# Hybrid attention/SSD layer on one core: GpSimd subtractions in four pieces, decay rows by a one-hot stationary column, next head pair's projections in the present group's tail

## The reference

```
h   = RMSNorm(x)
p   = h @ w_in          # q-latent 384 | kv-latent 256 | rope key 32 | z 2048 | x,B,C 4096 | dt 32 | gate_a 1024 | gate_b 1024
A   = latent attention: q = RMSNorm(q-latent) @ w_uq (16 heads of 64 + 32 rotary), k, v = RMSNorm(kv-latent) @ w_uk, w_uv,
      causal softmax for the prompt; for the samples over 2048 cached positions
B   = SSD: causal conv of width 4 and SiLU on x, B, C; per head cs = cumsum(dt * a) over chunks of 128 tokens;
      y = (C B^T * exp(cs_l - cs_s), s <= l) @ (x dt) + exp(cs_l) C state;  state = state * exp(cs_end) + B^T exp(cs_end - cs) x dt;
      samples: state = state * exp(dt a) + dt x B, y = C state;  y = RMSNorm(y * SiLU(z)) by groups of 256 channels
mix = (sigmoid(gate_a) * (A @ w_br_attn) + sigmoid(gate_b) * (B @ w_br_ssm)) @ w_out
x   = x + RMSNorm(mix);  x = x + RMSNorm(relu(RMSNorm(x) @ w_up)^2 @ w_down)
```

## Time and profile before

| | |
|---|---|
| median of 3 runs | 1798.62 us |
| the profiled execution: its own time, its span | 1798.48 us, 1796.4 us |
| PE, DVE, ACT, POOL busy | 86%, 56%, 29%, 27% of the span |
| TensorE's mean granted clock | 0.901 |
| opening and group 0 | 0 to 130 us |
| groups 1 to 8 | 130 to 1051 us |
| sample rows | 1051 to 1255 us |
| mixing projections, norms, MLP | 1255 to 1796 us |

### The profile page before, as it was taken

One profiled execution on the slowest core, in us unless ns is written; L12 is line 12 of the kernel. 1 busy time (PEld: TensorE's weight loads), 2 busy tenths in 40 slices (PEclk: granted clock), 3 DMA queues, 4 the chain that ended last, 5 costly groups with the idle time before them and its releaser, 6 DMA issues.

```text
span 1796.4 us, 28368 instructions
## 1 busy us (share of the span) xinstructions
PE 1536.7 (86%) x11696; PEld 1397.6 (78%) x11696; DVE 1005.7 (56%) x1834; ACT 512.5 (29%) x930; POOL 476.6 (27%) x196
## 2 busy tenths in 40 slices
PE   4799879888798888987977668999995899999995
PEld 4798777687787777876867457777995899999995
DVE  6577688688686877877868542333234422222225
ACT  3232323223233233232232222222222322222221
POOL 1232222121221212222112012222344244444441
PEclk9898989899899898998988669999897899999997
DMA  3133121121221211312213028884231222222221
GB/s 107 59 88 95 47 77 59 50 86 51 81 76 39 86 60 39 95 55 72 71 38 96 24 74 275 251 259 132 95 118 35 71 95 92 87 93 95 95 94 60
DMA packets 109586, 160.45 MB, mean 89 GB/s; under 512 B 16497, under 2 KB 83570, under 8 KB 109458
## 3 DMA queue, kind: packets, MB, share of 16 engines
q1 hardware_dynamic: 56594, 130.14, 22.5%
q10 hardware_dynamic: 52864, 28.51, 5.7%
HBM read 145.87 MB, written 12.74 MB: 88 GB/s over the span
## 4 chain that ended last, share of the span: by engine, by line
PE 61%; DVE 28%; issue 5%; ACT 3%; ACTq 2%; SPq 1%; POOL 1%; DMA 1%; DVEq 0%; POOLq 0%
PE lin L455 44%; PE Pb L486 2%; PE lin L494 2%; DVE csm L1294 2%; PE lin L601 2%; PE Pb L542 1%; DVE arena L1273 1%; DVE acc L1469 1%; PE Pb L583 1%; ACTq L1018 1%; PE lin L622 1%; DVE sm L1300 1%; PE Pb L580 1%; PE lin L568 1%; DVE arena L1331 1%
## 5 line engine op out<-in xcount | busy, mean ns | idle before, releaser
L413 POOL TENSOR_TENSOR w_lo<-w_stage,w_hi 128x1024 fp32r<-128x1024 f32 x184 | 464.5, 2525 | 1271.0 <-ACT w_hi L817 1271.0
L455 PE MATMUL lin<-act_hi,w_hi 128*128 128x260 f32 x1760 | 373.2, 294 | 19.6 <-DVE acc L1537 8.1
L455 PE MATMUL lin<-act_lo,w_hi 128*128 128x260 f32 x1760 | 362.4, 288 | 0.0
L455 PEld LDWEIGHTS lin<-act_hi,w_hi 128*128 128x128 f32 x1760 | 279.8, 195 | 28.9 <-issue 21.6
L455 PEld LDWEIGHTS lin<-act_lo,w_hi 128*128 128x128 f32 x1760 | 280.5, 195 | 0.0
L817 ACT ACTIVATE w_hi<-w_stage 128x1024 fp32r<-128x1024 f32 x184 | 193.9, 1054 | 243.1 <-PE lin L455 221.6
L455 PE MATMUL lin<-mid_hi,w_hi 128*128 128x260 f32 x1024 | 220.8, 299 | 41.6 <-DVE mid_lo L1458 18.8
L455 PE MATMUL lin<-act_hi,w_lo 128*128 128x260 f32 x1760 | 235.7, 287 | 0.0
L455 PEld LDWEIGHTS lin<-act_hi,w_lo 128*128 128x128 f32 x1760 | 221.9, 191 | 3.3 <-issue 3.3
L455 PE MATMUL lin<-mid_lo,w_hi 128*128 128x260 f32 x1024 | 216.5, 295 | 0.0
L455 PEld LDWEIGHTS lin<-mid_hi,w_hi 128*128 128x128 f32 x1024 | 168.8, 202 | 52.2 <-issue 32.6
(11 more groups left out here) (240 smaller groups left out, 2139.3 us busy)
## 6 DMA issues: line engine op xcount, KB each, us to landing
w_stage<-in_wall SPq DMA_DIRECT2D x184, 512.0 KB, 3.5
arena<-in_cache SPq DMA_DIRECT2D x124, 144.0 KB, 3.2
arena<-in_state ACTq DMA_DIRECT2D x16, 512.0 KB, 8.3
out_stateT<-arena ACTq DMA_DIRECT2D x16, 512.0 KB, 4.0
o_attn<-in_cache SPq DMA_DIRECT2D x64, 128.0 KB, 3.7
o_attn<-in_cache ACTq DMA_DIRECT2D x64, 128.0 KB, 4.0
arena<-in_xT SPq DMA_DIRECT2D x8, 520.0 KB, 5.4
out_yT<-arena SPq DMA_DIRECT2D x8, 260.0 KB, 2.0
```

The costliest lines, as they stand in the source:

```text
L413: pool.tensor_tensor(w_lo[:, slot, :], w_stage[:, slot, :], w_hi[:, slot, :].bitcast(F32), ALU.subtract).then_inc(S["w_split"], 1)
L455: mm = pe.matmul(lin[:, pl.slot, hf, 0:HALF], w[:, ch.slot, off:off + P], r[:, hf * HALF:(hf + 1) * HALF], start=(k == 0 and p == 0), stop ...
```

## The change

It has three parts.
1. GpSimd's subtraction of a chunk is four instructions of 128 x 256; the signal is on the last.
2. `csm`, `sdm` and their VectorE instructions go. TensorE spreads each head's row itself: the stationary operand is a column of the identity (one-hot over 32 partitions) repeated 128 times, the moving one the 32 x 128 chunk of `cs3`; four such matmuls take the place of the one of 512 columns, and four of 16 columns that of the one of 64.
3. uq0, uq1, uk, uv, ql of the next group stand in the present group's tail, with their chunks UQ and UKV ahead of SA and SB, and so do their read-outs on ScalarE (`heads_out`) and VectorE (`queries_out`, `keys_out`, `latents_out`).

```diff
-STEADY_LIN = HEAD_LIN + ["x0", "sA0", "x1", "bC", "sA1", "b", "sA2", "c", "sA3", "z0", "z1"] + TAIL_LIN
+STEADY_LIN = (["bB", "x0", "sA0", "x1", "bC", "sA1", "b", "sA2", "c", "sA3", "z0", "z1", "uq0", "uq1", "uk", "uv", "bc", "ql"]
+              + S_LIN)
-STEADY_CH = ["UQ", "UKV"] + IN_LIN + ["SA", "SB"]
+STEADY_CH = IN_LIN + ["UQ", "UKV", "SA", "SB"]
...
-                        pool.tensor_tensor(w_lo[:, slot, :], w_stage[:, slot, :], w_hi[:, slot, :].bitcast(F32),
-                                           ALU.subtract).then_inc(S["w_split"], 1)
+                        for q in range(4):
+                            part = slice(256 * q, 256 * q + 256)
+                            low = pool.tensor_tensor(w_lo[:, slot, part], w_stage[:, slot, part],
+                                                     w_hi[:, slot, part].bitcast(F32), ALU.subtract)
+                        low.then_inc(S["w_split"], 1)
...
+                def head_row(h):
+                    return ident[0:32, 4 * g + h:4 * g + h + 1].to_broadcast([32, P])
...
-                    pe.wait_ge(S["csm_ready"], g * 4 + (c + 1))
-                    pe.matmul(lin[:, pl.slot, 0, :], ones[0:32, :], csm[:, :, :], start=True, stop=True)
+                    for h in range(HPG):
+                        pe.matmul(lin[:, pl.slot, 0, h * P:(h + 1) * P], head_row(h), cs3[:, tok], start=True, stop=True)
...
                     values(u + 1)
+                if has_in:
+                    queries()
                 pe.wait_ge(S["o_ready"], g * 8 + 8)
                 pe.wait_ge(S["sqg_ready"], g * 2 + 2)
                 statistics(Pb[0:TOKT, 2, 0:8], sqg, 2).then_inc(S["g_stat"], 1)
+                if has_in:
+                    keys()
+                    value_rows()
                 pe.wait_ge(S["g_diag"], g + 1)
                 broadcast_stat(c_lin(i, "bc"))
+                if has_in:
+                    latent_queries()
...
+                def heads_out():
+                    round_chunk(c_chunk(i, "UKV"))
+                    for h in range(2):
+                        pl = c_lin(i, f"uq{h}")
+                        done(pl)
+                        act.activation(cols(Qt[0:64, h, :]), lin_cols(pl, 0, 64), ACT.Copy)
+                        act.activation(qbd_hi[64 * h:64 * h + 64, 8 * h:8 * h + 8],
+                                       lin[0:64, pl.slot, 1, HALF - NB:HALF], ACT.Copy).then_inc(S["qbd_hi_s"], 1)
+                    pl = c_lin(i, "uk")
+                    round_chunk(c_chunk(i, "UKV").next())
+                    done(pl)
...
-                    if c < NCH - 1:
-                        masked_decay(c + 1)
...
                 if has_in:
-                    z_gate((0,))
+                    z_gate((0, 1))
+                    queries_out(0)
+                    queries_out(1)
                 dve.wait_ge(S["g_stat"], g + 1)
                 inverse_rms(Pb[0:TOKT, 2, 0:8], 0.25 / (D_INNER // GROUPS), S["g_diag"])
                 if has_in:
-                    z_gate((1,))
-                    silu(0)
+                    keys_out()
                 pl = c_lin(i, "bc")
...
                 dve.wait_ge(S["state_out"], g * 16 + 16)
                 if has_in:
+                    latents_out()
+                    silu(0)
                     silu(1)
                     conv(2, 0)
```

More of the change, by code:

```diff
@@ L531, in project, with queries, keys, value_rows @@
                         linear(c_lin(i, name), c_chunk(i, name), K8, act_rhs(), between=between)
+                def queries():
+                    for h in range(2):
+                        linear(c_lin(i, f"uq{h}"), c_chunk(i, "UQ"), [k * 256 + h * P for k in range(3)],
+                               mid_rhs(0, 3), opens=(h == 0))
+                def keys():
+                    linear(c_lin(i, "uk"), c_chunk(i, "UKV"), [0, P], mid_rhs(3, 2))
+                def value_rows():
+                    ch, pl = c_chunk(i, "UKV"), c_lin(i, "uv")
+                    free_slot(pl)
+                    for c in range(NCH):
+                        for k in range(2):
+                            tok = slice(CHUNK * c, CHUNK * (c + 1))
+                            a, b = mid_hi[:, 3 + k, tok], mid_lo[:, 3 + k, tok]
+                            wh = w_hi[:, ch.slot, 512 + k * P:640 + k * P]
+                            wl = w_lo[:, ch.slot, 512 + k * P:640 + k * P]
+                            for n, (x, w) in enumerate(((a, wh), (a, wl), (b, wh))):
+                                mm = pe.matmul(lin[:, pl.slot, 0, c * P:(c + 1) * P], x, w,
+                                               start=(k == 0 and n == 0), stop=(k == 1 and n == 2))
+                    mm.then_inc(S["lin_done"], 1)
+                def latent_queries():
+                    ch, pl = c_chunk(i, "UKV"), c_lin(i, "ql")
+                    free_slot(pl)
+                    pe.wait_ge(S["lin_free"], c_lin(i, "uq1").index + 1)
+                    for k in range(2):
+                        out = lin[:, pl.slot, 0, 16 * k:16 * k + 16]
+                        for n, (w, r) in enumerate(((w_hi, qbd_hi), (w_hi, qbd_lo), (w_lo, qbd_hi))):
+                            mm = pe.matmul(out, w[:, ch.slot, 256 + k * P:384 + k * P], r[:, :],
+                                           start=(n == 0), stop=(n == 2))
+                    mm.then_inc(S["lin_done"], 1)
                 if not has_rest:
@@ L584, in scan_back @@
                               ).then_inc(S["y_done"], 1)
[L586 to L615, removed]
+                if g:
+                    pe.wait_ge(S["state_ready"], g * 4)
+                else:
+                    pe.wait_ge(S["rows_ready"], 1)
+                    pe.wait_ge(S["sp_ln"], 2)
+                for h in range(HPG):
+                    mm = pe.matmul(Pb[:, 3, 16 * h:16 * h + 16], head_row(h), cs3[:, SEQ:SEQ + 16], start=True, stop=True)
+                mm.then_inc(S["sdec_mm"], 1)
                 pe.wait_ge(S["xc_ready"], g * 4 + 4)
@@ L906, in finish_inputs @@
                         act.dma_start(sS[:, t], src.rearrange("b h p n -> (h p) b n")).then_inc(S[f"st_in{t}"], 16)
+                def heads_out():
+                    round_chunk(c_chunk(i, "UKV"))
+                    for h in range(2):
+                        pl = c_lin(i, f"uq{h}")
[6 more added lines that the diff above has]
+                    done(pl)
+                    act.activation(cols(Kt[0:64, 0, :]), lin_cols(pl, 0, 64), ACT.Copy).then_inc(S["k_act"], 1)
+                    pl = c_lin(i, "uv")
+                    done(pl)
+                    act.activation(V[:, 0:2, :], lin[:, pl.slot, 0, 0:256].rearrange("p (c v) -> p c v", c=2), ACT.Copy
+                                   ).then_inc(S["v_act"], 1)
                 if not has_rest:
@@ L916, in group @@
                     finish_inputs()
+                    heads_out()
                     return
@@ L1708, in weight_stream @@
             else:
-                group_rest(name, i - 1)
+                group_rest(name, i if name[0] == "U" else i - 1)
     for m in range(KT):
```

118 lines of the change are left out of this document (51 added, 67 removed).

## The result

The changed kernel takes 1769.91 us (median of 4 runs, 1765.16 to 1772.46) against 1798.3 for the kernel before beside it: ratio 0.9837, 95% interval 0.9803 to 0.9871. The profiled execution took 1770.81 us with a span of 1769.0.

A forecast was written before the change was run, and what follows sets the result against it. TensorE's own work was taken to bound the kernel, with its waits for VectorE to be gained. Terms -20.7 + 16.5 - 1.8 - 3.5 - 5.3 = -14.8 from 1798.5 gave 1784 us; own range 1773 to 1794, wider range 1752 to 1812.

The forecast's parts named there:

- 0.7, my choice: Scan steps: shorter waits leave TensorE's clock up for some more matmuls, 0.7 us a group.
- 0.5 for a clock that falls in the longer wait: Next group's head: TensorE's clock falls while it waits longer behind the late state loads, +0.5 us, six times.
- B: Tail, head and state loads: moved projections make s0 11.5 us later and the second state load 3.3 late; sum +16.5 us.
- C: Group 8, bounded by VectorE: three csm instructions (L1294) go, 0.6 us each, -1.8 us.
- D: Opening and first head: two to three blocks of VectorE, 2.0 to 0.5 us each, shorten; -3.5 us.
- the sums of the branch projection: Head: VectorE's L1273, held 2.78 us, meets a short block instead, -1.5 of TensorE's 2.15 us wait.
- A: Scan steps: TensorE waits less for VectorE once csm goes and holds shorten; -2.95 us a group, times 7, -20.7.
- E: Sample rows: 0.75 us of TensorE's 1.77 us wait behind L1503 goes, for seven rows, -5.3 us.
- Price of a piece: GpSimd's subtraction: a 128 x 256 piece takes 0.72 us, bounds 0.58 and 1.28; four take 2.9 instead of 2.34.
- cheaper tail: Rival, chance 0.25: small instructions of inverse_rms are not held, s0 8.8 us later, second load 0.6 late; 1762 us.
- No change: Rival, chance 0.20: tail takes 2.1 us more per group, so VectorE's savings are waited for at the loads; 1798 us.
- slower case: Rival, chance 0.15: GpSimd's pieces follow so closely that VectorE doesn't get in between; +30, 1829 us.

## Why the prediction was half right

The direction and the mechanisms stood; the sum was off by 13 us. **The step that failed is the price of TensorE's clock**: "0.7, my choice" for it in the scan steps, "0.5 for a clock that falls in the longer wait" in B, and nothing at all in C, D and the sums of the branch projection. A removed wait was priced at little more than its own length, and so was a new one. What the runs showed in its place stands below: 1.7 us a group instead of 0.7 in the scan steps, and 2.0 to 2.4 instead of 0.5 in B, in the other direction.

Without the move, the prediction's own terms are -20.7 - 1.8 - 3.5 - 5.3 - 7 x (1.5 + 1.6) = -53; the kernel without the move measured -61. The move by the same terms is +16.5 + 21.7 = +38; measured +32. By stage, from the two profiled executions:

| stage | forecast | measured |
|---|---|---|
| to the first `scan_front(0)` (D) | -3.5 | -7.4 |
| groups 1 to 7 (A, B) | -4.2 | -11.0 |
| group 8 (C) | -1.8 | -3.5 |
| sample rows and first mixing norm (E) | -5.3 | -6.9 |
| behind it | 0 | +1.6 |
| sum (rounded) | -14.8 | -27.3 |

**Price of a piece.** Right: 0.72 forecast; in the changed kernel the shortest of 736 takes 0.712 us and the median 0.735. GpSimd's own mean per chunk went to 3.1 us, and TensorE hardly waited for it (0.8 us in all, 0.7 before). Nor is that the +1.6 of the last stage: it arises right behind the mixing norm, where TensorE waits 3.5 instead of 3.2 us for `inverse_rms` and then stays at clock 0.50 for some 11 us instead of 8.

**A, scan steps.** The waits are right: 4.8 to 2.3, where 2.5 was forecast. The size is not: steps 1 and 2 lost 3.9 us, not 2.95. Over groups 1 to 7, TensorE's waits in these two steps fell from 33.9 to 18.9 us in all, 2.1 a group, for which the prediction had 2.25. But its busy time fell too, from 194.9 to 182.8 us, though the changed kernel has more matmuls there and not fewer: the granted clock of the two steps went from about 0.94 to 1.00. That is 1.7 us a group, where 0.7 was chosen.

**The sums and the head.** The same is seen there in the kernel with four pieces alone, which runs the same matmuls as the kernel before. In the rest of the period the waits fell from 29.8 to 20.2 us over the seven groups and the busy time from 240.6 to 228.8, at a clock of about 0.90 instead of 0.86. The prediction had only the waits.

**B, tail and loads.** The path through the tail is right step by step. uq0 starts 4.7 us behind L593, as forecast; s0 was forecast 11.5 later, and the tail is 11.2 longer. `inverse_rms` met the pieces and is 2.0 longer instead of 2.7 (5.1 us from 340.8 to 345.9; 3.1 before). The Trainium skill, page "SBUF — State Buffer", section "Who interferes with whom", says that the order of issue and not the shape of an instruction decides who is blocked; four instructions of 65 x 8 values, each held for 0.5 us, agree. One of them, L1161, has a single tensor as its input and took 0.71 us instead of 0.17. The loads were forecast 3.3 late and are 3.2. But "0.5 for a clock that falls in the longer wait" was far too small: step 0 went from 13.9 to 15.9 us, and against the kernel without the move from 13.5 to 15.9, so 2.4.

That the groups came out only 7 us off the forecast is luck, for larger misses cancel. Over the seven groups, tail and rest together were forecast at 6 x 1.7 + 3.3 = +13.5 us and measured +2.3, step 0 at +3 and measured +13.8, steps 1 and 2 at -20.7 and measured -27.2.

**C and D.** The first head went from clock 0.76 (28.1 us, from 130.0 on) to 1.00 (23.7 us, from 127.0 on), so the clock has a part in D as well. But these are single executions. The four kernels with short subtractions alone, which differ only in the place of the loads, reach the first `scan_front(0)` at 149.4 to 153.5 us, and group 8 scatters by more than C's whole term, as said under the table. Whether C's -1.8 and D's -3.5 were too small is not shown.

**E.** The mechanism is right: L1503 took up to 2.36 us and now takes 0.72 at most, where about 1 was forecast, and TensorE's waits ahead of that matmul fell from 7.8 to 1.9 us in all.

**The rivals.** The cheaper tail had the nearer time, 1762 against 1784, but not the cause: the small instructions are held, and the second load is 3.2 us late and not 0.6. No change fell. The slower case, starvation between pieces, is excluded: `csm` takes 1.21 us beside four pieces, and no VectorE instruction of the changed kernel takes more than 0.59 us longer than the shortest of its line and shape.

That the clock follows the wait, and not the move, is shown by the late loads without a move (step 0 at 0.83) and by the early ones with it (1.00). But the length of a wait alone does not give the price. In the kernel before, a wait of 1.68 us ahead of `scan_front(0)` is followed by a step 0 of 15.0 us and one of 1.72 by a step of 13.8; the six of 3.1 to 5.6 us in the changed kernel are followed by 15.1 to 17.0 us. What decides in between is open.

Also not settled is what costs the one-hot columns their 10 us beside short subtractions. The rest of the period is 1.9 us longer. TensorE's waits there are the same (20.2 and 20.1 us over the seven groups) and its busy time is 2.0 us a group longer. The eight small matmuls for `sdec` take 0.9 of that (11.0 us in eight groups against 4.0 for the two that they replace); the rest goes with a clock of about 0.87 instead of 0.90, and why it is lower is not shown.

## What to carry to other kernels

When one engine's long instruction can hold another's, cut it until a piece is about as long as the held instruction (here 0.72 and 0.67 us; half of that gave no more), and measure that edit alone first: here it was worth more than the three parts together. Before work is moved into an idle stretch, list what is queued behind it, transfers above all, and move these ahead of it: here two load instructions put some 30 us earlier were worth 40 us. Price a TensorE wait with the granted clock of the stretch behind it, not by its length alone.

## What the runs showed of the hardware

A hold of VectorE by GpSimd lasts at most as long as the one GpSimd instruction that it meets: the longest was 2.23, 1.11, 0.59 and 0.31 us where a subtraction takes 2.34, 1.26, 0.72 and 0.44. VectorE got in before the next piece each time, at every length of piece.

A busy TensorE needs 16.4 us for 105 matmuls behind a wait of 3.5 us, and 13.5 in the kernel with early loads: the granted clock of 0.81 is a mean over a stretch at 1.2 GHz (0.50 at 264) and one at 2.4 GHz (1.00 from 271 on).

A subtraction of 128 columns costs 0.44 us, so that eight take 3.6 us where one takes 2.34. This still hid under the passes over `w_hi`: TensorE waited 2.2 us in all for `w_lo` with eight pieces, 0.7 with whole subtractions.
